# Causal attention rewritten around transposed scores, inside a hybrid block of delta rule, pooling and attention

## The chip, the core and the metric

The program runs on one core of one Trainium2 chip. The metric is the device time of one execution in microseconds (us). TensorE (PE in the profile) does the matrix products, VectorE (DVE) and ScalarE (ACT) the elementwise work and the reductions, GpSimd (POOL) some small elementwise work, and SyncE (SP) issues almost all transfers.

## The reference

One layer of a hybrid block over 1024 tokens of width 1024, in float32. A projection feeds three mixers: a gated delta rule (4 heads of 128, chunks of 64 tokens), a multi-scale pool, and attention with 4 heads (queries and keys 96 wide, values 64 wide). Their outputs go through one output projection, and a gated feed-forward layer follows. The change touches the attention alone:

```python
def chunk_causal_attention(q, k, v):
    qf = q.astype(jnp.float32) * (dqk ** -0.5)
    for qs in range(0, s, Q_BLOCK):                     # Q_BLOCK = 128
        end = qs + Q_BLOCK
        scores = jnp.einsum('bqhd,bkhd->bhqk', qf[:, qs:end], kf[:, :end])
        q_chunk = (qs + jnp.arange(Q_BLOCK)) // CHUNK   # CHUNK = 64
        k_chunk = jnp.arange(end) // CHUNK
        mask = k_chunk[None, :] <= q_chunk[:, None]
        p = jax.nn.softmax(jnp.where(mask, scores, -jnp.inf), axis=-1)
        outs.append(jnp.einsum('bhqk,bkhd->bqhd', p, vf[:, :end]))
```

The delta rule, which runs beside it, is a chain over the tokens: each pair of chunks (128 tokens, all four heads at once) needs the state that the pair before it left.

## The kernel before

Until about 322 us of the span the kernel computes the input projection, tile by tile (`gemm`, L2001 to L2019: for each of eight k steps six products, with operands split into a high and a low float32r part). Beside its last tiles it prepares the delta rule; VectorE inverts the 32x32 blocks there (`base_inverses`, L1686 to L1702: 31 steps of two operations) and, in the middle of that, makes the low part of the last weight tile (`last_split`, L1681).

Then come the *rounds*, up to about 532 us. The heads of the attention and the 128-token pieces of the delta rule run together in them. Four rounds stand in the code: round 0 as straight code (`FIRST_ROUND`), rounds 1 to 3 as one hardware loop over `ORDER`. Each round does one head of the attention and two pieces of the delta rule, in two slots of buffers; slot 1 runs six stages behind slot 0. A piece has 14 stages, named `pre, qk, turn, m0, x1, yz1, x2, yz2, ks, tr, av, oms, on, ot`. One list sets the order on all engines; each engine walks the list and issues what it has to do for each entry, so that all queues hold the same sequence and wait for each other by counters.

Attention for one head is three kinds of entries, over query tiles `t` from 7 down to 0. The counts are per head:

- `att_s` (L2203 to L2220): scores of 128 queries against their `(t+1)*128` keys, as plain float32 products into banks 4 and 5, with the mask added to the last 128 keys by a 97th row of the contraction. VectorE then takes the row minimum (L1818; the scores are negated), and ScalarE the exponential with that minimum as its bias and the row sum read out beside it (L1300).
- `att_t` (L2221 to L2234): the 36 blocks of 128x128 probabilities are transposed on TensorE, up to four at a time into bank 6, and ScalarE copies them to `probsT` (L1306).
- `att_pv` (L2235 to L2248): products with the values into bank 7. At the end of a query tile VectorE inverts the row sum (L1822) and scales (L1825) into the place of the values.

There is one copy of `probs` and one of `probsT`. After the rounds TensorE transposes the attention output (L2264), and the output projection starts between the last stages of the delta rule (`AFTER_ROUNDS`).

SyncE issues the loads in a fixed order. For each round it is `load_chunk(0, i)`, the two halves of the next head's queries (L700), and `load_chunk(1, i)` (L686 to L695). The keys of all four heads lie in `kT` from the start.

Of the kernel before, what the change touches and what calls it, by code (L numbers as in the profile page):

```python
# [13 lines left out]
P = 128  # L31
# [25 lines left out]
BIG = 1.0e30  # L57
assert sum(DOWN_GROUPS) == HID_TILES and TT == 8 and HEADS == 4 and GDN_HEADS == 4
# [15 lines left out]
def hybrid_block(nc, e_d, a_d, diag_d, n_d, qkv_d, qk_d, x2_d, hid_d, hs_d, wt_d, x, positions, attn_norm, w_in, conv_w, a_log, dt_bias, gdn_out_norm, pool_w, pool_scale,  # L74
# [26 lines left out]
    le = c.take("le", [P, P])  # L101
    gt = c.take("gt", [P, P])
# [15 lines left out]
    row_stats = [c.take(f"row_stat{j}", [P, 4]) for j in range(2)]  # L118
# [21 lines left out]
    V = r.take("V", [P, TT, HEADS, V_DIM])  # L140
    kT = Region(r.at).take("kT", [P, HEADS, SEQ])
# [86 lines left out]
    qh = r.take("qh", [P, SEQ])  # L228
# [10 lines left out]
    probsT = [r.take("probsT0", [P, 4, P])]  # L239
    assert r.at <= R1 + 72 * KB  # L240
    r = Region(R1 + 96 * KB)
    probs = r.take("probs", [P, SEQ])
# [38 lines left out]
    with ctx:  # L281
# [61 lines left out]
        queries_loaded = [sem(f"queries_loaded{h}") for h in range(2)]  # L343
# [11 lines left out]
        kT_loaded = sem("kT_loaded")  # L355
        mask_rows = sem("mask_rows")
# [28 lines left out]
        q_tiles = list(range(TT - 1, -1, -1))  # L385
        groups_of = {t: (range(2) if t >= 4 else range(1)) for t in q_tiles}

        head_part = []
        for t in q_tiles:
            for g in groups_of[t]:  # L390
                head_part.append(("att_t", (t, g), 0))
                if t > 0 and g == groups_of[t][-1]:
                    head_part.append(("att_s", t - 1, 0))
                head_part.append(("att_pv", (t, g), 0))
        tp = Steps(sem("att_pe"), [f"s{w}" if st == "att_s" else f"{st[4:]}{w[0]}.{w[1]}" for st, w, _ in head_part],
                   ahead=True)
        ta = Steps(sem("att_act"), [n for t in q_tiles for n in ([f"e{t}"] if t < TT - 1 else []) + [f"p{t}.{g}" for g in groups_of[t]]],
                   ahead=True)
        td = Steps(sem("att_dve"), [f"{n}{w if st == 'att_s' else w[0]}" for st, w, _ in head_part
                                    if st == "att_s" or st == "att_pv" and w[1] == groups_of[w[0]][-1]  # L400
                                    for n in (("low",) if st == "att_s" else ("rinv", "o"))],
                   ahead=True)
        tp_first = Steps(sem("att_first_pe"), [f"s{TT - 1}"])
        ta_first = Steps(sem("att_first_act"), [f"e{TT - 1}"])
        td_first = Steps(sem("att_first_dve"), [f"low{TT - 1}"])
        pe_scores, act_exps, dve_lows = ([c_first if t == TT - 1 else c for t in range(TT)]
                                         for c, c_first in ((tp, tp_first), (ta, ta_first), (td, td_first)))
        HEAD_END = [(st, w, 1) for st, w, _ in head_part[-2:]]
        head_part = [("att_s", TT - 1, 0)] + head_part
# [5 lines left out]
        W_HIGH_AT, W_LOW_AT = (11, 15, 19, 23), (13, 17, 21, 25)  # L415
        ORDER = []
        for n, e in enumerate(chunk_part):
            ORDER += [e] + head_part[n * len(head_part) // len(chunk_part):(n + 1) * len(head_part) // len(chunk_part)]
            ORDER += [("w_high", W_HIGH_AT.index(n), 0)] if n in W_HIGH_AT else []
            ORDER += [("w_low", W_LOW_AT.index(n), 0)] if n in W_LOW_AT else []  # L420
        turn_end, values_end = HEAD_END
        scores_at = ORDER.index(("att_s", TT - 1, 0))
        assert ORDER[-2:] == head_part[-2:] and ORDER[scores_at + 2] == ("att_t", (TT - 1, 0), 0)
        ORDER = (ORDER[:scores_at] + [turn_end] + ORDER[scores_at:scores_at + 2] + [values_end] + ORDER[scores_at + 2:-2])
        SOLVE_FREE = ("pre", "qk", "turn")
        AT_ENTRY = [(st, b, 0) for st in SOLVE_FREE for b in range(2)]
        head_entry = [e for e in head_part if not e[2]][:3]
        AT_ENTRY = [e for n, e in enumerate(AT_ENTRY) for e in [e] + head_entry[n * 3 // len(AT_ENTRY):(n + 1) * 3 // len(AT_ENTRY)]]
        FIRST_ROUND = AT_ENTRY + [e for e in ORDER if not e[2] and e not in AT_ENTRY]
        AFTER_ROUNDS = [e for e in ORDER if e[2] and e not in HEAD_END]  # L430

        def moved(order, entry, ahead_of):
            rest = [e for e in order if e != entry]
            at = rest.index(ahead_of)
            return rest[:at] + [entry] + rest[at:]
# [139 lines left out]
        block = ctx.enter_context(nc.Block())  # L575


        qk_parts = qk_d.rearrange("h s p n -> (h s p n)").rearrange("(a p n) -> a p n", p=QK, n=BANK)
        qk_halves = qk_parts.rearrange("(h s) p n -> h s p n", s=4)

        @block.sync
# [1831 lines left out]
```

## Time and profile before

| | |
|---|---|
| three timed runs | 1272.95 us median, 1271.55 to 1273.26 |
| profiled execution, first to last instruction | span 1271.9 us |
| median of the runs less that span | 1.05 us |
| busy over the span | PE 1229.7 us (97%), PEld (weight loads) 1025.3, DVE 826.0 (65%), ACT 470.4 (37%), POOL 410.0 (32%) |
| chain that ended last | PE 69%, DVE 16%, issue 5%, POOL 3%, ACT 3%, DMA 2% |
| the stretch from 322.5 to 532.0 us | 209.5 us, PE busy 187.2, DVE 135.7, ACT 84.7, POOL 45.3 |

The profile gives one time for the profiled execution, its span; no time of its own around the span is given, so the last difference is to the median of the timed runs. Busy time counts each instruction to the end of its last result. TensorE issues the next product before that, so a busy TensorE is not one that issues without gaps: distances between the starts of products tell what a product costs in a stream. A plain float32 product shows as two records, a float32r product as one.

### The profile page before, as it was taken

How to read it: one execution, taken by the hardware profiler on the slowest of the kernel's cores; microseconds unless marked ns; L12 is line 12 of the kernel's file. 1: busy time of each engine (PE TensorE's matmuls, PEld its weight loads, DVE VectorE, ACT ScalarE, POOL GpSimd, SP SyncE). 2: the span in 40 equal slices, each digit the busy share in tenths (PEclk: the TensorE clock that was granted, in tenths of full speed). 3: DMA queues.
4: the chain of work that ended last, by engine and by line, in shares of the span. 5: the costliest groups of instructions: out<-in, count | busy, mean ns of one | idle time of the engine just before them, and what ended most of it. 6: DMA issues, size and time to landing. Idle time of an engine off the chain costs nothing.

```text
span 1271.9 us, 17471 instructions
## 1 busy us (share of the span) xinstructions
PE 1229.7 (97%) x6204; PEld 1025.3 (81%) x6204; DVE 826.0 (65%) x1260; ACT 470.4 (37%) x776; POOL 410.0 (32%) x371
## 2 busy tenths in 40 slices
PE   6999999999889999899999999999999999999999
PEld 5788777887778888888878888888888887888877
DVE  5446787885566766634575666565565579677776
ACT  5131332432243443324453333333333344344342
POOL 5001111243112221201664656565575456100000
PEclk9998999999899999999999999999999999999999
DMA  7311234455722321032414665653667349684545
GB/s 231 116 51 33 79 98 136 133 164 158 233 86 60 103 57 54 1 114 102 132 35 157 207 207 174 216 192 123 198 227 268 109 139 311 185 258 145 171 124 174
DMA packets 190886, 183.17 MB, mean 144 GB/s; under 512 B 19598, under 2 KB 146908, under 8 KB 190812
## 3 DMA queue, kind: packets, MB, share of 16 engines
q1 hardware_dynamic: 190688, 182.16, 45.4%
q8 instruction: 44, 0.72, 0.2%
q14 instruction: 30, 0.25, 0.1%
q10 hardware_dynamic: 124, 0.04, 0.0%
HBM read 124.50 MB, written 56.62 MB: 142 GB/s over the span
## 4 chain that ended last, share of the span: by engine, by line
PE 69%; DVE 16%; issue 5%; POOL 3%; ACT 3%; DMA 2%; SPq 0%; ACTq 0%; DVEq 0%; POOLq 0%
PE ps L2367 30%; PE ps L2372 13%; PE ps L2138 5%; PE ps L2278 5%; PE ps L2015 5%; DVE stage L1607 2%; PE ps L2245 2%; PE ps L1993 2%; PE ps L2214 2%; PE ps L2233 1%; DVE w_lo L1488 1%; DVE row_stat L1818 1%; DVE stage L1601 1%; POOL mla_sc L980 1%; DVE xop L1870 1%
## 5 line engine op out<-in xcount | busy, mean ns | idle before, releaser
L2367 PE MATMUL ps<-xop,wop_hi 128*128 128x512 f32 x1232 | 380.3, 390 | 1.7 <-ACT snap L1435 0.8
L2367 PEld LDWEIGHTS ps<-xop,wop_hi 128*128 128x128 f32 x1232 | 230.9, 188 | 51.1 <-issue 2.3
L2367 PE MATMUL ps<-xop,wop_lo 128*128 128x512 f32 x616 | 239.9, 389 | 0.0
L2372 PE MATMUL ps<-dop,wop_hi 128*128 128x512 f32 x440 | 136.3, 391 | 2.7 <-DVE x L1968 2.7
L2367 PEld LDWEIGHTS ps<-xop,wop_lo 128*128 128x128 f32 x616 | 115.7, 188 | 24.0
L1886 DVE TENSOR_TENSOR wop_lo<-w_sumS,wop_hi 128x512 fp32r<-128x512 f32 (+1 forms) x104 | 87.8, 846 | 68.7 <-ACT wop_hi L1368 68.7
L1886 DVE TENSOR_TENSOR wop_lo<-w_pair,wop_hi 128x512 fp32r<-128x512 f32 (+1 forms) x76 | 84.9, 1118 | 35.6 <-ACT wop_hi L1368 35.6
L2015 PE MATMUL ps<-act_hi,w_hi 128*128 128x512 f32 x320 | 104.3, 407 | 0.2 <-DVE stage L1607 0.2
L1968 DVE TENSOR_TENSOR x<-x,ps 128x512 f32<-128x512 f32 x112 | 76.7, 684 | 37.7 <-PE ps L2372 37.7
L2372 PEld LDWEIGHTS ps<-dop,wop_hi 128*128 128x128 f32 x440 | 81.9, 188 | 22.5 <-DVE wop_lo L1886 3.9
L2015 PE MATMUL ps<-act_lo,w_hi 128*128 128x512 f32 x320 | 99.6, 393 | 0.0
L2015 PE MATMUL ps<-act_hi,w_lo 128*128 128x512 f32 x320 | 99.6, 393 | 0.0
L2372 PE MATMUL ps<-dop,wop_lo 128*128 128x512 f32 x220 | 85.8, 390 | 0.0
L1368 ACT ACTIVATE wop_hi<-w_sumS 128x512 fp32r<-128x512 f32 (+1 forms) x104 | 63.2, 610 | 57.6 <-PE ps L2367 42.4
L2015 PEld LDWEIGHTS ps<-act_hi,w_hi 128*128 128x128 f32 x320 | 60.4, 191 | 16.2 <-issue 4.7
L2015 PEld LDWEIGHTS ps<-act_lo,w_hi 128*128 128x128 f32 x320 | 60.7, 190 | 12.9
L2015 PEld LDWEIGHTS ps<-act_hi,w_lo 128*128 128x128 f32 x320 | 60.6, 190 | 12.8
L1368 ACT ACTIVATE wop_hi<-w_pair 128x512 fp32r<-128x512 f32 (+1 forms) x76 | 46.4, 612 | 60.2 <-PE ps L2367 47.3
L1488 DVE TENSOR_TENSOR w_lo<-raw,w_hi 128x1024 fp32r<-128x1024 f32 x20 | 27.0, 1350 | 59.4 <-ACT w_hi L1180 59.4
L1084 POOL TENSOR_TENSOR w_sumS<-w_pair 128x512 f32<-128x512 f32 (+1 forms) x26 | 33.7, 1296 | 64.2 <-DVE wop_lo L1886 49.3
L2372 PEld LDWEIGHTS ps<-dop,wop_lo 128*128 128x128 f32 x220 | 41.3, 188 | 8.7
L1073 POOL TENSOR_TENSOR w_sumS<-w_pair,w_sumS 128x512 f32<-128x512 f32 (+1 forms) x26 | 35.9, 1379 | 34.5 <-DVE wop_lo L1886 34.5
(314 smaller groups left out, 2306.6 us busy)
## 6 DMA issues: line engine op xcount, KB each, us to landing
w_pair<-in_w_gate_up SPq DMA_DIRECT2D x44, 512.0 KB, 5.3
hidden<-up SPq DMA_DIRECT2D x22, 512.0 KB, 3.0
wd_rows<-in_w_down SPq DMA_DIRECT2D x22, 512.0 KB, 5.4
raw<-in_w_in SPq DMA_DIRECT2D x21, 512.0 KB, 4.4
wd_raw<-down_sums SPq DMA_DIRECT2D x12, 768.0 KB, 8.1
down_sums<-wd_rows SPq DMA_DIRECT2D x33, 256.0 KB, 2.6
wd_raw<-in_w_down SPq DMA_DIRECT2D x9, 768.0 KB, 7.8
qkv_kept<-qkv_st SPq DMA_DIRECT2D x12, 512.0 KB, 5.3
```

The lines of the kernel that those rows point to most:

```text
L1073: pool.tensor_tensor(w_sum["S4"][:, 0:kh, :], w_pair[n % 2][0][:, kh:2 * kh, :], w_sum["S2"][:, 0:kh, :], ALU.subtract).then_inc(sums_read ...
L1084: pool.tensor_tensor(s1, a21, a22, ALU.add).then_inc(sums_ready, 1)
L1368: act.activation(wop_hi[q % RING][:, 0:kh, :], src, ACT.Copy).then_inc(wop_high, 1)
L1488: dve.tensor_tensor(w_lo[slot][:, :, :], raw[rawslot][:, :, :], w_hi[slot][:, :, :].bitcast(f32), ALU.subtract).then_inc(raw_used, 1)
L1607: op = dve.scalar_tensor_tensor(dst[:, d:SEQ], src[:, 0:SEQ - d], tap(3 - d), dst[:, d:SEQ], ALU.mult, ALU.add)
L1886: dve.tensor_tensor(wop_lo[q % RING][:, 0:kh, :], src, wop_hi[q % RING][:, 0:kh, :].bitcast(f32), ALU.subtract).then_inc(wop_ready, 1)
L1968: dve.tensor_tensor(part, part, bank, ALU.add).then_inc(added, 1)
L2015: last = pe.matmul(ps[0:rows, pair + h, :], w[:, k, 0:rows], a[:, k, h * BANK:(h + 1) * BANK], start=(k == 0 and w is whi and a is a_hi), ...
L2138: last = pe.matmul(ps[:, out_bank, h * P:(h + 1) * P], lhs(h), rhs(h), start=True, stop=True)
L2278: last = pe.matmul(ps[:, op_pair[t] + h, :], o, w[:, k, h * BANK:(h + 1) * BANK], start=(k == 0 and len(parts) == 2 and w is w_out_hi), st ...
L2367: last = pe.matmul(ps[:, bank, :].rearrange("p (t n) -> p t n", n=P), w[:, k, :], a[:, k, :, :], start=(p in ("P1", "P2", "P7") and k == 0 ...
L2372: last = pe.matmul(ps[:, bank, :], w[:, k, :], a[:, k, :], start=(p in ("P1", "P2", "P7") and k == 0 and w is wop_hi[s] and a is hi), stop ...
```

## The change

The rounds become straight code with one list (`ORDER`) for all heads and pieces, and the attention is computed in another way:

- **Scores transposed.** Entry `st` computes, for a block of 128 keys `kt` and a group `g` of four query tiles, the transposed scores (keys on the partitions, up to 512 queries along the row). A head has 12 such units: 8 of group 1, 4 of group 0. ScalarE takes the exponential straight into one of four `expT` buffers, and entry `pv` uses those as stationary operand for the values. The transposes and the copies after them are gone.
- **Row minima apart.** The minimum of each query's scores is needed before the exponential, and along the partitions it can't be taken there. Entries `mx` compute untransposed scores once more, as float32r products into bank 4 (12 per head, up to 512 wide), VectorE takes the minimum of each, and `mr` (two per head) turns the four minima columns of a group into a row by four products of 128 columns with a stationary operand that is one column repeated. ScalarE copies that row, negated, into row 96 of the queries (`low_row`). A row of ones in the keys adds it.
- **Mask as rows.** Eight more rows of the contraction add the mask, so it is 105 rows long. SyncE builds them in DRAM early and loads them once.
- **Sums as a column.** The values have a 65th column of ones, so the row sums come out of the same product; VectorE inverts four of them at once and scales a group of four tiles at once, two pairs of operations per head for eight before.
- **Loads.** Keys and queries come one head at a time into two buffers (`load_head`), in four transfers.
- **Places.** The minima of head 0 stand inside the last two tiles of the input projection on TensorE, and between the steps of `base_inverses` on VectorE. Scores and values of head 0 then run as a whole, with only `pre`, `qk` and `turn` of the first two pieces among them; `m0` of the first piece comes after head 0. From there heads 1 to 3 are spread over the 100 remaining stages.

```diff
+            load_head(2)
+            for i in range(1, TT // 2):
                 load_chunk(0, i)
-                load_queries(i, 1, 4)
-                load_queries(i, 0, 0)
                 load_chunk(1, i)
+                if i == 1:
+                    load_head(3)
...
+            def load_head(h):
+                if h >= 2:
+                    sp.wait_ge(tp.sem, tp.after(f"s0.{3}", h - 2))
+                for half in range(HALVES):
+                    cols_h = slice(half * BANK, (half + 1) * BANK)
+                    sp.dma_start(keys_h[h % 2][0:QK, cols_h].bitcast(f32), k_d[h, half, :, :]).then_inc(head_loaded[h % 2], 16)
+                    sp.dma_start(qrys_h[h % 2][0:QK + 1, cols_h].bitcast(f32), q_d[h, half, :, :]).then_inc(head_loaded[h % 2], 16)
...
+        ENTRY_AT = (2, 9, 5, 11, 18, 20)
+        first_head = scores_and_values([0])
+        FIRST_PART = []
+        for n, e in enumerate(first_head):
+            FIRST_PART += [e] + [AT_ENTRY[j] for j, at in enumerate(ENTRY_AT) if at == n]
+        later = scores_and_values(range(1, HEADS))
+        ATT_REST = maxima(1)
+        for h in range(1, HEADS):
+            ATT_REST += spread(later[starts[h - 1]:starts[h]], maxima(h + 1) if h + 1 < HEADS else [])
...
+            upto = min(len(ATT_REST), -(-(n + 1) * len(ATT_REST) // (len(GDN_REST) - 4)))
+            ORDER += [e] + ATT_REST[done:upto]
...
+            def low_row(g, h):                                    # ScalarE
+                act.wait_ge(mp.sem, mp.after(f"mr{g}", h))
+                act.activation(qrys_h[h % 2][QK:QK + 1, g * BANK:(g + 1) * BANK], ps[QK:QK + 1, 4, :], ACT.Copy,
+                               scale=-1.0).then_inc(ma.sem, 1)
...
+                        act.activation(expT[u % 4][:, 0:n], ps[:, 5 + u % 2, 0:n], ACT.Exp, scale=-1.0).then_inc(ta.sem, 1)
...
+            def row_low(t, part, h):                              # VectorE
+                dve.wait_ge(mp.sem, mp.after(f"mx{t}.{part}", h))
+                n = min(BANK, (t + 1) * P - part * BANK)
+                to = part_low[:, part, t - 4:t - 3] if t >= 4 else q_low[:, t:t + 1]
+                dve.tensor_reduce(to, ps[:, 4, 0:n], axis=AX.X, op=ALU.min).then_inc(md.sem, 1)
...
+            LOWS_AFTER = (30, 28, 26, 25, 23, 22, 20, 18, 16, 15)
             def base_inverses():
+                for w in FIRST_LOWS[:2]:
+                    row_low(*w, 0)
...
+                    if k in LOWS_AFTER:
+                        row_low(*FIRST_LOWS[2 + LOWS_AFTER.index(k)], 0)
...
+            def maximum(entry):                                   # TensorE
...
+                    pe.wait_ge(md.sem, md.after("low{}.{}".format(*order[at - 1][1]), h))
+                if kind == "mx":
+                    last = pe.matmul(ps[:, 4, 0:n], qrys_h[h % 2][0:KROWS, t * P:(t + 1) * P],
+                                     keys_h[h % 2][0:KROWS, part * BANK:part * BANK + n], start=True, stop=True)
+                else:
+                    for j in range(4):
+                        last = pe.matmul(ps[:, 4, j * P:(j + 1) * P], q_low[:, 4 * w + j:4 * w + j + 1].broadcast_to([P, P]),
+                                         ident_r[:, :], start=True, stop=True)
...
+                        pe.matmul(ps[:, 5 + UNITS.index(b) % 2, 0:n], keys_h[i % 2][0:KROWS, kt * P:(kt + 1) * P].bitcast(f32),
+                                  qrys_h[i % 2][0:KROWS, first:first + n].bitcast(f32), start=True, stop=True).then_inc(tp.sem, 1)
...
+                            last = pe.matmul(ps[:, 7, at:at + V_DIM + 1], expT[UNITS.index(b) % 4][:, (t - first) * P:(t - first + 1) * P],
+                                             V[:, kt, i, :], start=(kt == 0 and t == first), stop=(kt == 4 * g + 3),
+                                             skip_group_check=True)
```

Three places show how the order moves. The first is VectorE at the start of `base_inverses` (`w_lo` is the low part of a weight tile, `ps` the bank of the minima products). Before:

```order
L1488 TENSOR_TENSOR w_lo<-raw,w_hi 128x1024
L1695 TENSOR_TENSOR solve_tmp<-u_base,n_base 128x31
L1698 TENSOR_TENSOR n_base<-n_base,solve_tmp 128x31
L1695 TENSOR_TENSOR solve_tmp<-u_base,n_base 128x60
L1698 TENSOR_TENSOR n_base<-n_base,solve_tmp 128x30x2
L1695 TENSOR_TENSOR solve_tmp<-u_base,n_base 128x87
L1698 TENSOR_TENSOR n_base<-n_base,solve_tmp 128x29x3
```

After:

```order
L1518 TENSOR_TENSOR w_lo<-raw,w_hi 128x1024
L1720 TENSOR_REDUCE part_low<-ps 128x1 x2
L1739 TENSOR_TENSOR solve_tmp<-u_base,n_base 128x31
L1742 TENSOR_TENSOR n_base<-n_base,solve_tmp 128x31
L1739 TENSOR_TENSOR solve_tmp<-u_base,n_base 128x60
L1742 TENSOR_TENSOR n_base<-n_base,solve_tmp 128x30x2
L1720 TENSOR_REDUCE part_low<-ps 128x1
L1739 TENSOR_TENSOR solve_tmp<-u_base,n_base 128x87
L1742 TENSOR_TENSOR n_base<-n_base,solve_tmp 128x29x3
```

Two reductions now stand ahead of the first step and ten more among the steps, five of them ahead of the low part of the last weight tile, which TensorE needs for the last tile of the projection.

The second is TensorE where the delta rule of the first piece starts (`N` is the inverse, `M`, `B`, `E`, `S` are operands of its stages, `kh` and `qh` keys and queries of head 1). Before:

```order
L2143 MATMUL ps<-ident,N 128x128 x3
L2233 MATMUL ps<-ident,probs 128x128 [waits att_act]
L2233 MATMUL ps<-ident,probs 128x128 x3
L2245 MATMUL ps<-V,probsT 128x64 [waits att_dve,att_act]
L2245 MATMUL ps<-V,probsT 128x64 x3
L2233 MATMUL ps<-ident,probs 128x128 [waits att_act]
L2233 MATMUL ps<-ident,probs 128x128 x2
L2138 MATMUL ps<-M,B 128x128 [waits gdn_dve0,gdn_act0,gdn_pool0]
L2138 MATMUL ps<-M,B 128x128 x3
L2214 MATMUL ps<-kT,qh 128x512 [waits att_act]
L2214 MATMUL ps<-kT,qh 128x128
```

After:

```order
L2208 MATMUL ps<-ident,N 128x128 x3
L2153 MATMUL ps<-kh,qh 128x512 [waits att_max_act,head_loaded1]
L2153 MATMUL ps<-kh,qh 128x512 [waits att_max_dve]
L2203 MATMUL ps<-M,B 128x128 [waits gdn_dve0,gdn_act0,gdn_pool0]
L2203 MATMUL ps<-M,B 128x128 x3
L2153 MATMUL ps<-kh,qh 128x512 [waits att_max_dve]
L2203 MATMUL ps<-N,qkvf 128x128 [waits gdn_act0]
L2203 MATMUL ps<-N,qkvf 128x128 x3
L2203 MATMUL ps<-qkvf,N 128x128 x4
L2153 MATMUL ps<-kh,qh 128x384 [waits att_max_dve]
L2203 MATMUL ps<-M,B 128x128 [waits gdn_dve0,gdn_pool0]
```

What stands between the stages of the first piece is now one minima product each, which waits for VectorE's reduction of the one before; 14 such entries stand among the first 12 stages.

The third is SyncE at the loads for the round after the first (`REGISTER_ALU` and `ISA` are the loop's address and wait instructions). Before:

```order
L688 DMA qkvf<-qkv_kept 128x12x128
L691 REGISTER_ALU
L692 ISA
L692 DMA E<-decay_kept 128x512
L693 ISA
L693 DMA N<-inverse_kept 128x512
L694 REGISTER_ALU
L695 DMA A<-keys_kept 128x512
L699 ISA
L700 ISA
L700 DMA qh<-qk_kept 96x512
```

After:

```order
L737 DMA N<-inverse_kept 128x512
L739 DMA A<-keys_kept 128x512
L656 DMA kh<-mla_keys_kept 96x512
L657 DMA qh<-queries_kept 97x512
L656 DMA kh<-mla_keys_kept 96x512
L657 DMA qh<-queries_kept 97x512
L732 DMA qkvf<-qkv_kept 128x12x128
```

The four transfers of head 3 stand ahead of the load of the third pair's first piece, and they wait until head 1 is through with its scores.

## Rows read from the trace of the kernel before

**Rows 1.** Windows, by engine: length, busy (instructions), TensorE's granted clock, DMA.

```profile
322.50:532.00 209.50, 187.19 (x1445) 169.54 (x1444) 135.66 (x299) 84.66 (x176) 45.29 (x38) 0.98 0.30 90
378.70:428.90 50.20, 46.27 (x371) 42.16 (x370) 33.73 (x72) 19.94 (x42) 11.96 (x10) 1.00 0.25 72
```

**Rows 2.** Waits of TensorE from 378.7 to 428.9 us.

```profile
PE ps L2233 <- ACT probs L1300: 2.8, 4, 1.2
PE ps L2245 <- ACT probsT L1306: 1.1, 2, 0.8
```

**Rows 3.** Timeline of TensorE: start, duration, line, operands, records.

```profile
303.32 0.61 PE L2015 MATMUL ps<-act_hi,w_hi 128*128 128x512 f32 x2
303.77 0.62 PE L2015 MATMUL ps<-act_lo,w_hi 128*128 128x512 f32 x2
...
402.26 1.02 PE L2214 MATMUL ps<-kT,qh 96*128 x2
403.12 0.39 PE L2218 MATMUL ps<-kT,qh 97*128 x2
403.34 0.56 PE L2245 MATMUL ps<-V,probsT 128*128 x4
...
440.38 1.00 PE L2245 MATMUL ps<-V,probsT 128*128 x8
441.22 0.61 PE L2143 MATMUL ps<-ident,N 128*128 128x128 f32 x4
441.67 0.60 PE L2233 MATMUL ps<-ident,probs 128*128 128x128 f32 x4
```

**Rows 4.** The same windows view, stretches of 4 us around the start of the rounds.

```profile
328.00:332.00 4.00, 1.83 (x16) 1.74 (x16) 3.77 (x12) 2.77 (x3) 0.29 (x1) 0.76 1.10 332
332.00:336.00 4.00, 3.74 (x18) 3.74 (x19) 1.18 (x4) 0.80 (x3) 2.94 (x3) 0.50 1.04 186
```

**Rows 5.** VectorE, 330 to 545 us, by form: count, busy, mean ns, idle before.

```profile
L1776 DVE TENSOR_TENSOR E<-Vn,E 128x512 f32<-128x512 f32 x8 | 7.8, 980 | 0.3
L1774 DVE TENSOR_TENSOR E<-ps,decays 128x512 f32<-128x512 f32 x8 | 5.5, 688 | 11.3 <-PE ps L2138 11.3
L1818 DVE TENSOR_REDUCE row_stat<-ps 128x1 f32<-128x512 f32 x4 | 2.8, 689 | 0.1
```

**Rows 6.** Timeline of VectorE in the block inverses.

```profile
304.66 0.21 DVE L1695 TENSOR_TENSOR solve_tmp<-u_base,n_base 128x31 f32<-128x31 f32 x1 [9.55 <-DMA u_base<-blocks_kept]
309.65 1.22 DVE L1488 TENSOR_TENSOR w_lo<-raw,w_hi 128x1024 fp32r<-128x1024 f32 x1
318.77 0.42 DVE L1695 TENSOR_TENSOR solve_tmp<-u_base,n_base 128x252 f32<-128x252 f32 x1
329.08 0.48 DVE L1724 MEMSET S<- 128x512 f32 x1
```

**Rows 7.** Timeline of ScalarE at the start of the rounds.

```profile
322.56 1.02 ACT L1259 ACTIVATE sgT<-ps 128x1024 f32<-128x1024 f32 x1 [9.85 <-PE ps L2015]
328.51 1.28 ACT L1300 ACT_TABLE_LOAD   x1
333.41 0.60 ACT L1306 ACTIVATE probsT<-ps 128x512 f32<-128x512 f32 x1 [1.21 <-PE ps L2233]
```

**Rows 8.** ScalarE, 330 to 545 us, by form.

```profile
L1300 ACT ACTIVATE probs<-ps,row_stat 128x512 f32<-128x512 f32 x4 | 2.7, 687 | 11.4 <-DVE row_stat L1818 11.4
```

**Rows 9.** Timeline of SyncE's queue.

```profile
329.10 5.67 SPq L713 DMA_DIRECT2D inverse_kept<-n_base x4
337.35 0.83 SPq L718 DMA_DIRECT2D N<-inverse_kept x2
```

**Rows 10.** Transfers over the span: count, size, median us from issue to landing.

```profile
qkvf<-qkv_kept SPq DMA_DIRECT2D x8, 768.0 KB, 5.2
N<-inverse_kept SPq DMA_DIRECT2D x8, 256.0 KB, 3.1
qh<-qk_kept SPq DMA_DIRECT2D x8, 192.0 KB, 2.6
```

More of the change, by code:

```diff
@@ L227, in hybrid_block @@
     qk_gain = Region(r.at).take("qk_gain", [P, 2, QK])
-    qh = r.take("qh", [P, SEQ])
+    expT = [None, None] + [r.take(f"expT{j}", [P, BANK]) for j in (2, 3)]
+    bigs = r.take("bigs", [P, CHUNK])
     assert r.at <= SBUF_END, r.at - SBUF_END
@@ L238, in hybrid_block @@
     S_ = r.take("S", [P, 4, P])
-    probsT = [r.take("probsT0", [P, 4, P])]
+    expT[0] = r.take("expT0", [P, BANK])
     assert r.at <= R1 + 72 * KB
-    r = Region(R1 + 96 * KB)
-    probs = r.take("probs", [P, SEQ])
+    r = Region(R1 + 98 * KB)
+    expT[1] = r.take("expT1", [P, BANK])
     E_ = [E0, r.take("E1", [P, 4, P])]
@@ L403, in hybrid_block @@
[L403 to L409, printed above, removed]
+        GROUPS = (1, 0)
@@ new lines, in spread, with scores_and_values @@
+        def spread(first, second):
+            out = []
+            for n, e in enumerate(first):
+                out += [e] + second[n * len(second) // len(first):(n + 1) * len(second) // len(first)]
+            return out
+        def scores_and_values(heads):
+            units = [(u, h) for h in heads for u in UNITS]
+            order = [("st", *units[0])]
+            for before, now in zip(units, units[1:]):
+                order += [("st", *now), ("pv", *before)]
+            return order + [("pv", *units[-1])]
@@ L429, in hybrid_block @@
[L429 to L435, printed above, removed]
-        ACT_ORDER = moved(ORDER, ("av", 1, 1), ("oms", 1, 1))
+        AT_ENTRY = [(st, b, 0) for st in ("pre", "qk", "turn") for b in range(2)]
+        GDN_ALL = [(st, b, rnd - back) for rnd in range(TT // 2) for st, b, back in chunk_part if rnd >= back]
@@ L438, in hybrid_block, with vn_squares_late @@
+        assert len([e for e in ORDER if e[0] == "w_low"]) == 2 * TT and done == len(ATT_REST)
+        def vn_squares_late(order):
+            out = list(order)
+            for e in order:
+                if e[0] == "av" and e[1] == 1 and ("oms", 1, e[2]) in out:
+                    out.remove(e)
+                    out.insert(out.index(("oms", 1, e[2])), e)
+            return out
+        ACT_ORDER = vn_squares_late(ORDER)
         OP_EARLY = [(t, k) for half in range(2) for t in range(2) for k in range(half * 4, half * 4 + 4)]
@@ L1313, in _ @@
[L1313 to L1316 removed]
+                        act.activation(w_out_hi[:, k, half], w_out_sb[:, k, half], ACT.Copy).then_inc(w_out_high, 1)
+            for s in range(2):
+                act.wait_ge(qkv_kept[s], 16 * QKV_TILES // 2)
+            stages(ACT_ORDER)
             def o_split_high(t, ks):
```

387 lines of the change are left out of this document (185 added, 202 removed).

## The prediction

> **What bounds the kernel now.** I read the windows first. The stretch that the change touches is 209.5 us long, and TensorE is busy for 187.2 of it, VectorE for 135.7 and ScalarE for 84.7 [rows 1]. So TensorE sets the pace, and 22.3 us are open idle time. The waits of one middle round say what it waits for: 2.8 and 1.1 us, all of it the attention's own chain, the exponentials ahead of the transposes and the copies ahead of the values [rows 2]; no wait of the delta rule is in that list. The reader is to see that the rounds are a stream of products with short holes, that the holes belong to the attention, and that the delta rule's own latencies are covered by attention products.
>
> Busy time hides a part: a product's record runs on after the next could start. So I count work by distances between starts [rows 3]. A 512-wide float32 product takes 0.86 us (402.26 to 403.12) and a 128-wide one 0.22 (403.12 to 403.34), that is 0.217 per 128 columns on the mean; four value products take 0.84 (440.38 to 441.22), 0.21 each; four transposes 0.45, 0.11 each; two float32r products 512 wide 0.45, 0.227 each. A head has 36 blocks of 128x128, each once in the scores, the transposes and the values: 36 x (0.217 + 0.21 + 0.11) = 19.3 us. A piece of the delta rule has 48 products at 0.22 and 16 transposes at 0.11, 12.4 us. A round is then 2 x 12.4 + 19.3 = 44.1 us of 50.2 [rows 1], and 6.1 us are not work. For the stretch: eight pieces less the late part of the last (20 products and 4 transposes, 4.8 us) are 94.4, four heads 77.2, the 16 transposes at the end 1.8, together 173.4 us. Of 209.5 us, 36.1 are no work. That is what there is to win, and the sum below is made the same way.
>
> **The work of TensorE after.** Scores and values stay 36 blocks per head: 36 x 0.427 = 15.4 us (65 columns instead of 64 in the values are nothing; 105 rows instead of 96 neither, since 97 rows cost the same 0.22 [rows 3]). The transposes go, 4.0 us per head. The minima come: six products 512 wide at 0.227, 1.4 us; six narrower ones, 1536 columns together, for which no float32r row stands. At the 512's rate they are 0.7 us, at the float32 rate 2.6. Eight products for the two rows per head, 128 wide: as transposes 0.9 us, as float32 products 1.8. Ends 3.0 and 5.8 us per head; I take 3.6, nearer to the float32r row, since the operands are of that kind. In the Trainium skill, "TensorE: Matmul & The Clock Gate", section "LDWEIGHTS (loading the stationary operand)", a weight load takes as long as its columns at 1.2 GHz, 107 ns for 128; a narrow product with a new stationary operand would then not go below that, and by this rule the eight row products would be 0.9 us, my lower end; no run so far shows one.
>
> So the attention's work falls from 19.3 to 19.0 us per head: the change is no saving of work. Work after: 94.4 + 1.8 + 61.6 in the rounds, 3 x 3.6 for the minima of heads 1 to 3, and 3.6 for head 0's, which now stand in the projection: 172.2 us for 173.4. All of the result is decided by what the waits come to.
>
> **The new waits, from the projection on.**
> 1. *Projection.* Block inverses start at 304.66, and the low part of the last tile ends at 310.9, just ahead of TensorE, which needs it at 311.1 [rows 6]. Now two minima stand ahead of the first step; their products come at about 303 and 304.4 (third and fourth k step, 1.36 us each, six products at 0.227), so the inverses start at 305.4. Five reductions stand ahead of the low part, three of them after the start. With 0.69 us for 512 columns [rows 5] and 0.4 to 0.55 for the narrower the low part ends at about 314.2, while TensorE arrives at 312.5 (1.2 us of minima in this tile): wait 1.8. In the last tile three minima find their reduction late by 0.2 to 0.7, 1.3 together. I take 3.1 us; ends 1 and 5. The projection ends at 328.3 rather than 322.5. The inverses end at about 336.4 rather than 329.1.
> 2. *First exponential.* The table load of 1.28 us comes after the last gate tile's 1.02 [rows 7] and now stands between the first scores and their exponential: 329.4, 330.7, 331.4, while TensorE has two units (1.74 us) to do from 328.3. Wait 1.4 us. Before, it lay beside VectorE's work.
> 3. *Head 0 as a whole.* A unit is at most 1.7 us on TensorE against an exponential of 0.69 [rows 8], so ScalarE keeps ahead. Only the change of group waits for VectorE's scaling: 0.5 us. Its 15.4 us cover what came late: the inverse goes through DRAM, 11 us from the last step to the landing (329.1 to 337.8, then 3.1 [rows 9, 10]), 347.5 us now; `m0` comes at 328.3 + 1.4 + 0.5 + 15.4 + 5.2 (products and turns of two pieces) = 350.8. Covered by 3 us; if the transfers take longer than that it is the next to show.
> 4. *The run of minima.* Between the first 12 stages stand 14 entries of head 1's minima, with no scores or values. A minimum's turn is the product's drain, a reduction of 0.69, and whatever VectorE has ahead of it, 0.69 to 0.98 for an operation of the delta rule [rows 5]; only 0.9 to 1.8 us of a stage's products cover it. And the first piece's stages stand one after the other: TensorE waits for ScalarE's copy of 0.60 [rows 7] or VectorE's 0.69 with 0.2 us of minima beside it. Walking the list: the first two minima 0.9, four stages of the first piece 0.45 to 0.6 each (2.1), the two minima after `ks` 2.0 (three operations of the piece are ahead), the row 0.3, the last three minima and the row 1.0, 1.1 and 1.5. Together 9 us; ends 4 and 14. This is what I see as the price of the layout.
> 5. *Clock.* Where TensorE stood idle for more than half of 328 to 332 us, the granted clock fell to 0.50, that is 1.2 GHz, for the 4 us after [rows 4]; it cost about 2 us there. That place goes, but the run of minima is idle for a third of some 25 us. I take 2.5 us; ends 0 and 6.
> 6. *Head 3's load.* Its four transfers wait for head 1's last scores, then about 3 us of issue and 2.6 to landing [rows 10], against 4.9 us of work before the first minimum of head 3; and the next piece's 768 KB, 5.2 us, now stand behind them. I take 2.5; ends 0 and 6.
> 7. *The 84 stages between.* Attention's own holes go: scores run one unit ahead of the values, and four `expT` buffers stand where one was. But per stage there are 0.55 us of attention now. I take 1.5 us a round, 4.5, between none and the 6.1 of now (18).
> 8. *End.* The last four stages have no attention beside them, 1.3 us; the turn of the output and its copies as before, 1.3.
>
> Sum of waits 26.1 us for 36.1. After: 172.2 + 26.1 = 198.3 us for 209.5, that is -11.2. VectorE loses no time that counts: per head its reductions take 6.7 us instead of 6.1, its scalings some 1.2 instead of 3.5; ScalarE loses the copies. The straight code removes the loop's address work, for which no wait shows; I cost it at nothing. The profiled span lies 1.05 us below the median of the runs; made against the span, 1271.9 - 11.2 = 1260.7, and with that distance 1261.8. Prediction: 1262 us.
>
> **Rivals.**
> - *The delta rule's and the minima's waits stay covered (0.25).* For it: no delta rule wait in [rows 2], though attention stands between most stages only singly. Then point 4 is 4 us, 5 and 6 nothing, 7 and 8 together 3: 172.2 + 3.1 + 1.4 + 0.5 + 4 + 3 + 1.3 = 185.5, 24 us less, 1249. Against it: the minima are a chain through two queues that the kernel before did not have.
> - *The narrow float32r products cost as float32 (0.15).* Then 2.2 us more per head, 8.8 in all, of which none is hidden in head 0 and in the run: 1262 + 8.8 = 1271, which is no change. Against it: the operands' kind; for it: only 512-wide rows stand in the trace.
> - *Slower: every minimum waits (0.12).* One mechanism: bank 4 is the only one for minima, and TensorE's next one is queued in order behind the reduction. If the 28 entries of heads 2 and 3 wait as the first 14 do, 9 us for 14, it is 18 us more, and TensorE's list holds the scores and stages behind them: 1280. It decides where a turn (0.27 + 0.69, and 0.69 or more queued) exceeds the work between two minima, 2 to 3.5 us in the later list. For it: VectorE was busy 33.7 of 50.2 us in a round. Against it: that spacing.
> - The forecast (0.48), by itself 1255 to 1268.
>
> **How the numbers follow.** No change is within 0.2%, 2.5 us, about what a measurement can tell: 1270.4 to 1275.5. Faster: the forecast, the first rival and the better half of the second, 0.79. Same: 0.09, slower 0.12. All ends together at their low side give about 1245, at their high side 1289; I leave out one in ten on either side: 1248 to 1277.
>
> **What would show it.** Right: the waits of TensorE for `probs` and `probsT` gone; a wait for `w_lo` of about 2 us ahead of the last tile; waits of the minima products for VectorE's reductions, packed into the first 25 us after `m0`, with `m0` at about 351 us and the granted clock below 1 there; a hole at head 3's first minimum. Wrong: minima waits spread over all rounds (the slower rival), row products with starts 0.2 us apart (the second), or `m0` waiting for its inverse.

## The result: 1306.0 us, slower by 2.6%

The kernel after took 1305.99 us (median of 4 runs, 1305.27 to 1306.69) against 1272.65 for the one before in the same session: ratio 1.0264, 95% interval 1.0251 to 1.0278. Forecast were 1262 us and a range of 1248 to 1277. The time is outside the range, on the wrong side. The profiled execution has a span of 1303.8 us.

### The profile page after: what moved, and what is told of

It reads as the page before. It is cut to its first block, busy times and chain, and to the rows that moved or that the text cites. A ratio compares the mean times of both kernels' runs of the same rounds, so it can differ in the third digit from the quotient of the medians.

```text
span 1303.8 us, 16515 instructions
## 1 busy us (share of the span) xinstructions
PE 1234.7 (95%) x6092; PEld 1018.8 (78%) x6092; DVE 819.9 (63%) x1232; ACT 449.3 (34%) x720; POOL 404.1 (31%) x370
## 4 chain that ended last, share of the span: by engine, by line
PE 68%; DVE 15%; DMA 4%; issue 4%; SPq 4%; POOL 3%; ACT 2%; ACTq 0%; DVEq 0%; POOLq 0%
PE ps L2407 30%; PE ps L2412 14%; PE ps L2203 5%; PE ps L2047 5%; PE ps L2318 5%; DVE stage L1637 2%; PE ps L2025 2%; DMA qh<-queries_kept 1%; PE ps L2277 1%; SPq L751 1%; PE ps L2289 1%; DVE w_lo L1518 1%; POOL mla_sc L1021 1%; DVE stage L1631 1%; DVE wop_lo L1918 1%
## 5 line engine op out<-in xcount | busy, mean ns | idle before, releaser
L1338 ACT ACTIVATE expT<-ps 128x512 f32<-128x512 f32 (+3 forms) x48 | 23.4, 489 | 71.7 <-PE ps L2277 71.6
```

## The profile after

The waits of TensorE over the whole span, largest first (line, what it waited for, us in total, times, longest):

```profile
PE ps L2153 <- DMA qh<-queries_kept: 14.9, 1, 14.9
PE ps L2208 <- DMA N<-inverse_kept: 11.6, 1, 11.6
PE ps L2010 <- DVE prep L1482: 9.2, 1, 9.2
PE ps L2153 <- DVE part_low L1720: 8.0, 4, 5.2
...
PE ps L2153 <- DVE q_low L1720: 2.5, 4, 1.1
PE ps L2203 <- DVE M L1813: 2.4, 4, 0.7
...
PE ps L2289 <- ACT expT L1338: 1.8, 2, 1.3
```

The waits for `probs` and `probsT` [rows 2] are gone, as forecast. In their place stand two single holes, both for a transfer, and a third of 5.2 us that looks like VectorE's. (L2010's 9.2 us stand near the start of the kernel, where the change has no part; the kernel before waits 9.7 us there too.) The three in TensorE's timeline (start, duration, line, in brackets the idle time ahead and who ended it):

```profile
312.89 0.69 PE L2153 MATMUL ps<-kh,qh 105*128 105x384 f32 x1 [5.19 <-DVE part_low L1720]
...
370.21 1.12 PE L2208 MATMUL ps<-ident,N 128*128 128x128 f32 x4 [11.58 <-DMA N<-inverse_kept]
...
465.81 0.80 PE L2153 MATMUL ps<-kh,qh 105*128 105x512 f32 x1 [14.94 <-DMA qh<-queries_kept]
```

The first hole is a transfer's too. VectorE's timeline there shows the block inverses starting at 311.27 and not at 304.66 as in [rows 6], because `u_base` came late; the reduction that TensorE needs stands behind the first of their steps:

```profile
304.74 0.69 DVE L1720 TENSOR_REDUCE part_low<-ps 128x1 f32<-128x512 f32 x1 [0.94 <-PE ps L2153]
311.27 0.20 DVE L1739 TENSOR_TENSOR solve_tmp<-u_base,n_base 128x31 f32<-128x31 f32 x1 [5.84 <-DMA u_base<-blocks_kept]
```

So one reads SyncE's queue, where all three transfers are issued (start, time of the issue, line, transfer):

```profile
284.49 1.15 SPq L657 DMA_DIRECT2D qh<-queries_kept  x1
285.68 7.87 SPq L643 DMA_DIRECT2D qkv_kept<-qkv_st  x1
...
307.11 0.32 SPq L722 DMA_DIRECT2D u_base<-blocks_kept  x1
...
346.11 0.92 SPq L657 DMA_DIRECT2D qh<-queries_kept  x1
347.08 17.52 SPq L751 DMA_DIRECT2D inverse_kept<-n_base  x4
367.24 0.81 SPq L756 DMA_DIRECT2D N<-inverse_kept  x2
...
447.36 0.47 SPq L657 DMA_DIRECT2D qh<-queries_kept  x1
447.87 6.82 SPq L732 DMA_DIRECT2D qkvf<-qkv_kept  x1
454.73 8.78 SPq L736 DMA_DIRECT2D E<-decay_kept  x1
```

Behind each second load of queries the queue hangs: single issues take 7 to 9 us, and the four of `inverse_kept` 17.52 together, which took 5.67 in [rows 9]. What the DMA engines do meanwhile is in the windows (the last two columns are their mean busy share and GB/s):

```profile
450.00:452.00 2.00, 0.86 (x9) 0.72 (x7) 1.23 (x4) 0.44 (x1) 0.00 (x0) 1.00 0.07 26
452.00:454.00 2.00, 0.00 (x0) 0.00 (x0) 0.65 (x2) 0.00 (x0) 0.00 (x0) 1.00 0.07 26
...
460.00:462.00 2.00, 0.00 (x0) 0.00 (x0) 0.00 (x0) 0.00 (x0) 0.00 (x0) 0.50 0.07 26
```

They are not loaded. A share of 0.07 is about one engine of 16 (0.0625), at 26 GB/s. It doesn't fill the whole hole: from 456 to 458 us, when `qkvf` gets through, the share is 1.07, and from 460 to 464 it is at 0.06 to 0.07 again. The same low share stands from 288 to 294 and from 348 to 352 us. The last row shows also what follows: by then the granted clock is at 0.50, that is 1.2 GHz. Behind the second hole it still is when TensorE comes back:

```profile
370.00:376.00 6.00, 4.74 (x16) 3.64 (x17) 1.88 (x3) 1.20 (x2) 0.87 (x1) 0.50 0.91 348
```

**The theory (T1).** The change loads the queries with 97 rows instead of 96, so that the row for the minima comes as zeros. 97 is prime. If a transfer is shared out by whole rows among a number of engines that divides the rows, 96 rows get all 16 engines and 97 get one. In the Trainium skill, "DMA: Bandwidth & Descriptors", section "Why a DMA increments its semaphore by 16 and not by 1", the number of engines is the largest one up to 16 that divides the slowest dimension of both sides, with 100 partitions on 10 engines and 127 on one. The windows above agree with it (a share of 0.07 while a load of 97 rows is on its way), and experiment 3 measures the other row counts. **Rivals:** too many bytes ahead in the queue (R1), and the layout itself, its chain of minima through two engines (R2).

## Experiments

**1. Only the 97 rows.**

```diff
-    sp.dma_start(qrys_h[h % 2][0:QK + 1, cols_h]..., q_d[h, half, :, :]).then_inc(...)
+    sp.dma_start(qrys_h[h % 2][0:QK, cols_h]..., q_d[h, half, 0:QK, :]).then_inc(...)
+    sp.dma_start(qrys_h[h % 2][QK:QK + 1, cols_h]..., q_d[h, half, QK:QK + 1, :]).then_inc(...)
```

> The kernel after, with each 97-row load of the queries written as one transfer of 96 rows and one of a single row; bytes, queue, order and all arithmetic stay. Theory T1 (a transfer of 97 rows is carried by one DMA engine, at the 26 GB/s that the windows of after show, 7.5 us for 194 KB, two in a row per head, and what stands behind it on the queue waits): the hole of 11.6 us before m0 falls under 3, the one of 14.9 us before head 3's first minimum to under 4, u_base lands about 6 us earlier so that the 5.2 us before the low part goes to under 2; together 27 to 31 us less, 1275 to 1280 us. Rival R1 (too much stands in the queue ahead of the inverse and of head 3): the same bytes in the same order, so both holes stay within 2 us of 11.6 and 14.9 and the time within 3 us of 1306. Rival R2 (the layout itself, minima as a chain through two queues): also unchanged at 1306.

Measured: 1274.08 us (12 runs, 1267.31 to 1283.38), 31.9 less than after, a little more than the 27 to 31 expected; 1.0012 of before, interval 0.9989 to 1.0036, so without the holes the new kernel is as fast as before and no faster. None of the three holes is left; TensorE's waits from 325 to 532 us (its lines stand one further down than after's):

```profile
PE ps L2154 <- DVE part_low L1721: 3.1, 3, 1.6
PE ps L2204 <- DVE M L1814: 2.4, 4, 0.7
PE ps L2154 <- DVE q_low L1721: 2.2, 3, 1.1
PE ps L2204 <- ACT qkvf L1324: 2.0, 6, 0.4
PE ps L2290 <- ACT expT L1339: 1.8, 2, 1.3
...
PE ps L2154 <- DMA qh<-queries_kept: 0.5, 1, 0.5
```

The same bytes in the same order: R1 and R2 fall, T1 stands. `u_base` is issued at 299.33 instead of 307.11, `N` at 345.27 instead of 367.24. The spread of 16 us is new (before: 1269.95 to 1273.72 in 17 runs) and is taken up in experiment 5.

**2. Only head 0's loads.** The same edit, for `h == 0` alone.

> The same edit for head 0's two loads alone; heads 1 to 3 keep their 97-row loads. T1: only what stands behind head 0's loads moves, that is the load of u_base and with it the inverses: the 5.2 us before the low part goes; the hole before m0 gets at most as much shorter as its SyncE queue comes earlier, and stays above 6 us; the hole before head 3's first minimum stays at 14.9. 1298 to 1303 us. R1 and R2: 1306, no change.

Measured: 1299.01 us (1296.41 to 1301.37). The hole in the projection is gone; that before `m0` is 8.1 us and that before head 3's first minimum 15.1, since heads 1 to 3 still load 97 rows. The loss is spread over the places as the theory says: 7 us hang on head 0, 25 on the others.

**3. The rows by themselves.** The kernel before, with loads added behind its last store, each waited for; the distance to the next issue is the time of one. It was executed once.

```diff
+ sp.dma_start(qh[0:r, 0:BANK], rows_flat[0:r, :]).then_inc(queries_loaded[0], 16)
+ sp.wait_ge(queries_loaded[0], ...)
```

> The kernel before, with loads of DRAM rows of 2 KB added behind its last store, one at a time and each waited for: 96, 97, 128, 127, 112, 100, 98, 99, 64, 61, 48, 47, 9, 8 and 7 rows, then pairs without a wait between them (97+97, 97+96, 96+96, 96+1). T1, if the number of engines is the largest number up to 16 that divides the rows: 96, 128, 112, 64 and 48 rows land in 2 to 3 us, 97 and 127 in 8 to 10, 61 in 5 to 6, 47 in 4 to 5, 98 (14 engines) and 99 (11) in about 3, 100 (10) in about 3; the pair 97+97 takes twice a single one if both get the same engine, and the same as a single one if not; 97+96 ends with the 97. R1: the time goes by the bytes alone, 97 rows within 0.2 us of 96 and 127 within 0.2 of 128.

SyncE's timeline. L930 to L936 are 96, 97, 128 and 127 rows, L948 to L952 are 61, 48 and 47; L938 and L954 show where the last of each ends:

```profile
1270.95 0.35 SPq L930 DMA_DIRECT2D qh<-qk_kept  x1
1273.38 0.30 SPq L932 DMA_DIRECT2D qh<-qk_kept  x1
1283.58 0.36 SPq L934 DMA_DIRECT2D qh<-qk_kept  x1
1286.24 0.23 SPq L936 DMA_DIRECT2D qh<-qk_kept  x1
1298.93 0.32 SPq L938 DMA_DIRECT2D qh<-qk_kept  x1
1301.46 0.29 SPq L940 DMA_DIRECT2D qh<-qk_kept  x1
...
1312.15 0.23 SPq L948 DMA_DIRECT2D qh<-qk_kept  x1
1319.54 0.32 SPq L950 DMA_DIRECT2D qh<-qk_kept  x1
1321.54 0.23 SPq L952 DMA_DIRECT2D qh<-qk_kept  x1
1327.55 0.27 SPq L954 DMA_DIRECT2D qh<-qk_kept  x1
```

| rows of 2 KB | 96 | 97 | 128 | 127 | 100 | 99 | 98 | 64 | 61 | 48 | 47 |
|---|---|---|---|---|---|---|---|---|---|---|---|
| largest divisor up to 16 | 16 | 1 | 16 | 1 | 10 | 11 | 14 | 16 | 1 | 16 | 1 |
| us | 2.4 | 10.2 | 2.7 | 12.7 | 2.9 | 2.7 | 2.5 | 2.6 | 7.4 | 2.0 | 6.0 |

Not in the table: 112 rows took 2.5 us, and 9, 8 and 7 rows 1.5 to 1.6. The four primes lie on one line: from 47 to 127 rows 6.7 us for 80 rows, 0.083 us a row, 24.5 GB/s, beside a fixed part of about 2 us. That is longer than the 8 to 10 us expected for 97 and 127 rows, and than the 5 to 6 and 4 to 5 for 61 and 47. All others take 2 to 3 us. Of the pairs without a wait between them, 97 and 97 rows took 18.5 us together (1332.19 to 1350.70). That is about 194 rows at 0.083 us and the fixed part, so they share the same engine. The pair of 97 and 96 took 10.9, where two of 96 took 3.2: what comes behind ends with it. By bytes alone, 97 would have been within 0.2 us of 96. Large transfers whose largest divisor is between 2 and 9 were not measured.

**4. The converse.** The kernel before, its 96-row loads of queries written as 89 rows and 7.

```diff
-  sp.dma_start(qh[0:QK, cols_h], ...)
+  for r0, r1 in ((0, 89), (89, QK)):
+      sp.dma_start(qh[r0:r1, cols_h], ...)
```

> The converse in the kernel before: each of its 96-row loads of the queries written as one of 89 rows and one of 7; bytes, order and arithmetic stay. T1: 89 rows go through one engine, about 7 us instead of 2.6; head 0's stand ahead of 768 KB of keys and the first chunk in the projection's last tile, the others come at the end of a round, just ahead of their use: 3 rounds by 4 to 8 us and 0 to 8 at the start, 12 to 30 us slower, 1285 to 1303. R1 and R2: the kernel before is within 1 us of 1272.7.

Measured: 1281.29 us, ratio 1.0075 (1.0063 to 1.0088). Slower by 9 us, by this alone. The size was below the 12 to 30 expected: the loads at the rounds' end cost 2.9 us in three waits and not 4 to 8 each. The rest is at the start of the rounds, in transfers that stand behind head 0's loads. None of these three waits is in the trace of before; against them, the waits for `probs` are 2.7 us shorter:

```profile
PE ps L2216 <- DMA kT<-qk_kept: 5.8, 1, 5.8
PE ps L2145 <- DMA N<-inverse_kept: 3.0, 1, 3.0
PE ps L2216 <- DMA qh<-qk_kept: 2.9, 3, 1.2
```

**5. The clock.** The forecast was 1262 us, and with the three holes closed the kernel still takes 1274. Its 12 times follow its mean clock: 1267.3 and 1267.5 at 0.996, 1271.6 and 1272.9 at 0.992, 1282.6 and 1283.4 at 0.984 and 0.982. Its windows from 326 us:

```profile
326.00:330.00 4.00, 2.83 (x9) 1.32 (x7) 3.65 (x11) 3.13 (x5) 0.00 (x0) 1.00 0.32 93
330.00:334.00 4.00, 3.87 (x19) 3.35 (x20) 3.59 (x13) 1.68 (x4) 0.00 (x0) 0.76 1.06 335
334.00:338.00 4.00, 4.00 (x16) 3.00 (x14) 1.88 (x6) 0.60 (x1) 0.00 (x0) 0.50 1.14 313
...
342.00:346.00 4.00, 4.00 (x16) 3.23 (x14) 0.00 (x0) 1.21 (x3) 0.00 (x0) 0.50 0.51 75
```

Ahead of the fall stands one hole of 1.3 us, the wait for the first exponential and its table (point 2); then the clock is at 0.50 for some 17 us although TensorE is busy throughout. Before, the falls lasted 3 to 7 us ([rows 4] is the first). So I filled the hole, after a wait that keeps bank 4 from being overwritten before ScalarE has read it:

```diff
+  if (g, kt, i) == (1, 0, 0):
+      pe.wait_ge(ma.sem, ma.after("row0", 0))
+      for _ in range(5):
+          pe.matmul(ps[:, 4, :], qrys_h[0][0:KROWS, 0:P], keys_h[0][0:KROWS, 0:BANK], ...)
   gafter(ta, f"e{g}.{kt}")
```

> The kernel e1_split97 with five float32r products of 512 columns (results not used) in the hole of 1.3 us in which TensorE waits for the first exponential, just behind the projection. In e1_split97 the granted clock is 0.50 to 0.52 from 332 to 348 us, right behind that hole, though TensorE is then busy throughout; its mean clock over 12 runs lies between 0.982 and 0.996 and its times between 1267.3 and 1283.4, the lower the clock the longer. Theory C (the fall belongs to that hole): the clock stays at 1.00 up to m0, mean clock 0.994 or more in every run, times 1266 to 1268 and close together, 6 to 8 us under e1_split97's median. Rival (the fall comes from the float32r minima or from the low load of the last tile, or is not to be had by filling): the clock falls as before, 1274 with the same spread.

Measured: 1266.88 us (7 runs, 1264.88 to 1270.61), clock 0.995 to 0.997, ratio to before 0.9964 (0.9950 to 0.9978). Five products of no use make the kernel 7 us faster, and its windows show why:

```profile
326.00:330.00 4.00, 4.00 (x15) 2.45 (x13) 3.69 (x10) 3.13 (x4) 0.00 (x0) 1.00 0.32 90
330.00:334.00 4.00, 3.85 (x22) 2.71 (x22) 3.59 (x13) 1.88 (x4) 0.00 (x0) 1.00 1.03 333
334.00:338.00 4.00, 4.00 (x33) 3.52 (x31) 2.11 (x9) 0.92 (x2) 1.01 (x1) 1.00 1.15 316
```

From 334 to 338 us TensorE has 33 records instead of 16. The hole makes the fall likely, not certain. In the traces of `e2_first_only` and `e8_minima_early` the clock is at 0.50 for 7 us behind the same hole, in that of the unfilled kernel with other addresses (`e5_place`, experiment 7) it stays at 1.00, and so it does in the kernel after itself (a line of TensorE's timeline and the window around it):

```profile
338.55 1.10 PE L2289 MATMUL ps<-V,expT 128*128 128x65 f32 x8 [1.30 <-ACT expT L1338]
338.00:342.00 4.00, 3.45 (x20) 2.66 (x21) 3.62 (x12) 2.10 (x4) 0.00 (x0) 1.00 1.09 330
```

So these 7 us are not in the 1306 as they stand; they came in with the kernel of experiment 1. That the hole also makes the spread of the 12 runs is likely but not shown, since only one of them has a trace; for it speaks that the 7 filled runs lie within 6 us.

**6. The run of minima (point 4).** Head 1's minima moved into the second half of head 0, one behind each of its last 14 entries, and for that head 1's load into the projection; the two edits were not run apart.

```diff
+            FIRST_PART += maxima(1)[n - 10:n - 9] if n >= 10 else []
-        ATT_REST = maxima(1)
+        ATT_REST = []
```

> The kernel e1_split97 with head 1's minima no longer between the delta rule's first stages but between the second half of head 0's scores and values (one behind each of its last 14 entries), and head 1's load moved ahead, behind the first chunk's in the projection. Term 4 of the prediction (9 us of waits in the run of minima, 8 measured in after): if right, 5 to 7 us of these go, since VectorE stands idle in head 0 (0.5 us busy from 338 to 348), and with the holes some of the clock's fall at 382 us; 1266 to 1270. Rival (the waits there belong to the delta rule's own chain, which then stands without cover): the stages behind m0 wait the same 8 us or more, 1273 to 1276.

Measured: 1265.27 us (1264.56 to 1270.72), ratio 0.9946 (0.9933 to 0.9959), 8.8 less than experiment 1. The waits from 325 to 532 us add up to 11.6 instead of 17.0. Those for the minima (`part_low` and `q_low`) are 3.4 us instead of 6.2, those of the delta rule's own chain (`M`, `qkvf`) about as before:

```profile
PE ps L2205 <- DVE M L1815: 2.3, 3, 1.2
PE ps L2155 <- DVE q_low L1722: 2.3, 2, 1.7
PE ps L2205 <- ACT qkvf L1325: 1.8, 4, 0.8
...
PE ps L2291 <- ACT expT L1340: 1.3, 1, 1.3
PE ps L2155 <- DVE part_low L1722: 0.9, 3, 0.6
```

So 5.4 of the 8.8 us are waits, within the 5 to 7 expected; the runs' clock was higher too (0.993 in four of five).

**7. The last stretch.** This is a second question, not one of the forecast's steps. From the output projection's first product to the end the code is the same, but the traces show 738.1 us in before and 741.9 in after. The small columns of the new kernel move all large buffers by 32 bytes. One kernel moves them on by 96, to the same remainder by 128 as in before; one moves those of before by 32.

```diff
+    c.take("gap", [P, 24])    # in experiment 1's kernel; [P, 8] in the kernel before
     R1 = c.at
```

> The kernel e1_split97 with 96 bytes of unused space per partition behind the small columns, so that every large buffer starts 32 bytes past a multiple of 128, as in the kernel before (in after and e1_split97 it is 64 past one). In the traces the stretch from the first product of the output projection to the end lasts 738.1 us in before and 737.1 in e4_before_89, but 741.9 in after, 742.0 in e2_first_only and 742.5 in e1_split97, with the same code. Theory P (the place of the buffers): that stretch comes back to 737 to 739 us, the time falls by 3 to 4 us from e1_split97's 1274.1, to 1270 to 1271. Rival (it is not the place, but what the rounds leave behind, or chance): the stretch stays at 741 to 743 and the time within 1.5 us of 1274.

Measured: 1277.58 us (12 runs, 1268.28 to 1282.61), last stretch 743.4. Not what theory P said. The spread is that of experiment 1, and at equal clock the two kernels' times agree within some 2 us (at 0.989 1277.6 and 1275.7, at 0.984 1282.2 and 1282.6).

> The kernel before with 32 bytes of unused space in the same place, so that its large buffers stand 64 bytes past a multiple of 128, as in after. Theory P: its last stretch goes from 738.1 to 741 to 742 us, the time from 1272.2 to 1275 to 1276. Rival: no change, within 1 us.

Measured: 1276.25 us, ratio 1.0037 (1.0025 to 1.0049), last stretch 741.3. So 32 bytes alone cost the kernel before 3.8 us, as P said, though the remainder by 128, with which P explained it, is not the rule (`e5_place`). One of the six runs shows a mean clock of 0.942 and took 1279.55 us, only 3 more than the others, so a mean clock does not by itself give a time. The next kernels put the buffers at exactly the old addresses, by laying `q_low` over a buffer that is free by then, beside both edits of 5 and 6:

> Both edits on e1_split97: the five filling products of e7_fill and the early minima of e8_minima_early. e8's waits of TensorE from 300 to 532 us come to about 13 us for e7's 18; e8 ran at clock 0.993 with falls at 330, 348 and 366 us. If the filled hole keeps the clock up there as in e7 and nothing else changes, 4 us of clock come back, 1260 to 1262. Rival: the falls at 348 and 366 stay, since they follow holes of their own behind head 0's minima: 1263 to 1265.

> e9_both with q_low laid over a small buffer that is free by then, so that the large buffers stand at exactly the addresses of the kernel before. e6_before_place lost 3.8 us by a shift of 32 bytes (its last stretch 741.3 us for 738.1), yet e5_place, shifted by 128 from before's place, kept 743.4. Theory P2 (only before's own place is the good one, a rule of more than 128 bytes): last stretch 737 to 739 us, the time 3 to 4 us under e9_both. Rival (the loss of the last stretch comes with the changed kernel, and e6's has another reason): 741 to 743, within 1 us of e9_both.

Measured: 1266.27 us (1265.45 to 1268.66) and 1263.44 (1261.63 to 1265.63); last stretches 740.8 and 739.3. For the second, 1263.44 is 2.8 us under the first, where P2 said 3 to 4. The first was no better than its parts: the fall at 330 was closed, but a longer one stood behind the minima in head 0, its windows from 342 us:

```profile
342.00:346.00 4.00, 3.02 (x18) 2.42 (x19) 2.15 (x5) 0.28 (x1) 2.24 (x2) 1.00 0.51 152
346.00:350.00 4.00, 3.81 (x10) 2.07 (x8) 2.32 (x5) 0.60 (x1) 0.00 (x0) 0.54 0.85 323
```

> e7_fill with q_low laid over the free buffer, so that the large buffers stand where they stand in the kernel before; the minima of head 1 stay between the delta rule's first stages. If the place is worth the 2.8 us that e10_both_place gained over e9_both: 1263 to 1265, last stretch 739 to 740 us. If that gain was chance: 1266 to 1267.

> e10_both_place with each of head 1's minima two entries earlier in head 0, so that they stand between larger units (from about 336 us, when VectorE has just finished the inverses). In e9_both four minima wait 0.2 to 0.6 us between 343 and 349 us and the clock falls there to 0.50 for some 16 us. If these holes make the fall, and the earlier place closes them: mean clock 0.994 or more, 1259 to 1261. If VectorE isn't free in time, the first of them wait instead: 1263 to 1266.

Measured: 1265.83 us (1263.40 to 1266.71) for the first, between the two expectations, 1.0 under `e7_fill` with intervals that overlap, last stretch 738.9; 1263.51 (1262.34 to 1264.88) for the second, the same as `e10_both_place` and not the 1259 to 1261 of the idea tested, clock 0.991 to 0.993. The fall came only 0.6 us later than in `e10_both_place` (at 347.0 for 346.5) and lasted 10 us instead of 14; one wait of 0.56 us still stands ahead of it. Over the traces the last stretch is 737.1 to 739.3 us with the old addresses (five kernels) and 740.8 to 743.4 with others (eight; experiment 1's 742.5 holds a fall of the clock of 3.4 us). That the addresses matter is shown by `e6_before_place`; by which rule, and through which engine, stays open.

The fastest are `e10_both_place` and `e12_two_sooner`: 0.9927 (0.9913 to 0.9940) and 0.9930 (0.9918 to 0.9941) of before. They beat both kernels.

## Why the prediction was wrong

**The step that failed** is the price of the queries' load. Points 3 and 6 took every transfer at its duration in [rows 10], 2.6 us for 192 KB, and never priced the one row more that the diff adds. With 97 rows a load takes 10.2 us by itself, two in a row 18.5, and what stands behind them on the queue waits. In point 3 "covered by 3 us" became a hole of 11.6; in point 6 a term of 2.5 became 14.9; in point 1 `u_base` came 6 us late, which the sum had not at all. The three holes are 31.7 us, and behind each of them TensorE works at a clock of 0.50 for a while. By experiment 1 the one row costs 31.9 us, a net number, since the fall of experiment 5 came in when the holes went. The condition "if the transfers take longer than that it is the next to show" was right. [rows 10] has only transfers of 96 and 128 rows; that none of 97 was there should have made the price a term with bounds. With the loads split, point 6's wait is 0.5 us for the 2.5 forecast.

**The clock (point 5)** was given 2.5 us, behind the run of minima. There it did fall: it is at 0.65 from 398 to 402 us in after and at 0.50 from 374 to 378 in `e7_fill`. Once the holes are closed, the larger loss lies behind the wait of point 2, which was itself forecast to the tenth (1.4, measured 1.30) but priced as a wait alone: 7 us on the median (experiment 5).

**Not in the sum** is the last stretch, some 3 us longer in the traces by the addresses (experiment 7). In whole times the old addresses gave 1.0 to 3.8 us, for the filled kernel 1.0, which is not clear of the noise. From after over `e1_split97` and `e7_fill` to `e11_fill_place` the steps are 31.9, 7.2 and 1.0 us, 40 of the 44 between 1306 and 1262. The other 3.8 stay open.

**What held.** In `e7_fill`, where the holes are closed and the clock does not fall up to there, `m0` stands at 350.2 us for a forecast of 350.8. In experiment 1 the projection ends at 326.9 for 328.3: point 1's waits are 1.2 us (0.9 of them for `w_lo`) and not 3.1. Point 4's run of minima had 7.5 us of waits in after for 9, between 372.5 and 396.1 us. The narrow float32r products cost what was taken, so the second rival falls. In experiment 1's projection a minimum of 512 columns adds 0.26 us (0.24 to the next start, and 0.02 on the six products behind it, which take 1.36 us without one), one of 384 columns 0.21, one of 128 0.14. Four row products add 0.47, 0.12 each, which is not below the 107 ns that the prediction names. With 0.17 us for 256 columns, an estimate between its neighbours, that is 3.5 us per head for 3.6. Points 2, 3, 4, 7 and 8 were to be 18.0 us, and experiment 1's trace lists 17.0 us of waits, but the two are not the same measure: the forecast counts all that is not work, 36.1 us in before, where the trace lists 22. The output projection starts 7.0 us earlier in `e7_fill` than in before (526.85 for 533.82), not 11.2. The slower rival named minima that wait all through: they don't. The result was slower, but by a mechanism that no rival held.

**In the prediction's sums** two things are off, and neither changes what is said above. "All ends together" leaves out the ends of the minima's work (3.0 and 5.8 us per head); with them it is 1243 and 1298, not 1245 and 1289. The first rival adds 1.3 us for the end although it has "7 and 8 together 3".

## What to carry to other kernels

Count the rows of every transfer that a change touches, and look at their largest divisor up to 16; one row more or less can cost four times the transfer and hold up all that is queued behind. A DMA share near 0.06 during a wait for a transfer is its mark in a profile. Price a hole on TensorE by what the clock does after it as well. Where it can't be closed, try filling it with products: alone that gave 7 us here, beside the early minima nothing (`e9_both` 1266.27, `e8_minima_early` 1265.27), since the clock then fell behind the next holes. And compare a stretch that the change does not touch before crediting or charging the change with the whole difference.

## What the runs showed of the hardware

- Rows on one DMA engine: 24.5 GB/s, 0.083 us per 2 KB row; two such transfers in a row use the same engine (18.5 us for 2 x 97 rows).
- The issuing queue itself hangs behind two of them: 6.8 to 8.8 us for an issue that takes 0.3 to 0.4 in experiment 1.
- Behind a hole of 1.3 us the granted clock fell to 0.50 for 7 to 17 us of full work in three traces, and stayed at 1.00 in two. Over 24 runs of two kernels (`e1_split97`, `e5_place`) each thousandth of mean clock went with 1.16 us; the run of `e6_before_place` at 0.942 does not follow that.
- 32 bytes of shift of all large buffers made the kernel before 3.8 us slower.
